# One transformer chain on one core: where the perceptron loop turns, who makes two chunks' low parts, and two small reorderings

## The chip, the core and the metric

One Trainium2 chip, one NeuronCore. The metric is the device time of one execution in microseconds (us). The work of a core is spread over TensorE (PE in the profile; its weight loads are PEld), VectorE (DVE), ScalarE (ACT), GpSimd (POOL) and SyncE (SP, which here only issues DMAs). They run side by side and wait for each other on semaphores.

## The reference

Two blocks of two layers each, 512 latent tokens (and 256 context tokens in the first block), width 1024, all in float32. Cut to what the change touches:

```python
# first block, layer i: attention (neighbourhood, then sliding window), then
h = h + ga1 * (attention(modulate(rms_norm(h, g), sh1, sc1)) @ wo)
h = h + ga2 * (jnp.square(jax.nn.relu(modulate(rms_norm(h, g), sh2, sc2) @ w1)) @ w2)
# second block, layer 0 (even mixer): differential attention y_a and an mLSTM y_b
hm = mlstm_chunkwise(q, k, v, i, f) * jax.nn.sigmoid(o)
y_b = rmsnorm(hm, ml_head_g) * jax.nn.silu(z)
h = h + rmsnorm(concat(y_a, y_b) @ w_out, post_g)
```

## The kernel before

The residual stream stays in SBUF as `m.h`, 8 tiles of 128 features by up to 768 tokens. The program is a row of stages, each a block in which every engine has its own stream of instructions, with a barrier of all engines between two of them: a prologue, neighbourhood attention (`na_stage`), the first perceptron (`mlp_stage`, layer 0, 768 tokens), sliding-window attention (`swa_stage`), the second perceptron (`mlp_stage`, layer 1, 512 tokens), differential attention, `mlstm_stage` and `odd_stage`.

**Precision and chunks.** Each big product is three matmuls (`mm3`, L284 to L286): high part by high part, low by high, high by low. So each weight chunk (128 x 2048) is loaded by SP into one of two slots of `raw`; ScalarE copies it to `wh` (`split_hi`, L238: the high part) and GpSimd subtracts (`low_part`, L245, four pieces of 512 columns: `wl = raw - wh`). TensorE waits for the low part. The last two chunks handled in a stage already belong to the stage that follows: at a stage's end the low part of slot 0 was GpSimd's (`coming.low(pool, 0)`, or `split_lo(pool, m, 0, 0)` in `swa_stage`) and that of slot 1 is VectorE's (`coming.low(dve, 1)`, `split_lo(dve, m, 1, 1)`), in the same four pieces.

**The perceptron.** 16 blocks of 256 hidden features. An "up" projection (letters a, b, c, d, in two tiles t = 0, 1) makes `lin[t] = w1 @ u`; ScalarE makes `relu` from it (L740, step `e_g t`) and its square's high part `hid_hi` (L743), VectorE the square (L835) and its low part (L839, step `lo_g t`). A "down" projection (x, y, v, w, eight tiles n) multiplies by `w2`, and VectorE adds each tile to the residual (L848, step `e_g n`). TensorE needs bank `lin[n % 2]` back from two tiles earlier, so up tile t after a down waits for `e_y6`, `e_y7`. The order is a, then seven rounds of b x c y, then d v w.

**Counting steps.** `Steps` turns a step's name into a semaphore value. In a loop it is `i * len(body) + const`, and for a step of the round before (`back = 1`) one body less. In round 0 "the round before" is not there: the value then is whatever lies one body length under the named step.

```python
up("b", i * 4 + 1, 1, i, lambda t: [(A, f"e_a{t}", ()), (D, f"e_y{6 + t}", (i, 1))])
```

VectorE's body has 24 steps and 4 steps ahead of it (`s_a0, lo_a0, s_a1, lo_a1`). So in round 0 the wait for `e_y6` of the round before is a wait for VectorE's third step, `s_a1`, and that for `e_y7` one for the fourth.

**A stage's end** (`Stats`). After the last down (w) or output projection, each residual tile k is squared by ScalarE as soon as VectorE has added to it (L357; from k = 3 on it waits for GpSimd's sum number k - 2, whose buffer it reuses), GpSimd adds squares 1 to 5 (L364), and TensorE sums the sum and squares 6 and 7 over the features with a matrix of ones (`Stats.sum`, L373). ScalarE then splits the chunk in slot 1 and makes the root (L379, L381). TensorE fills up with matmuls that nobody reads (`keep_busy`, L292). Then comes the barrier, and VectorE starts to scale the next stage's input.

**The start of `swa_stage`.** Small projections share two PSUM banks in turn (`Linear`): entry n of the list `order` needs its bank back from entry n - 2. For the first keys: a sum of squares for the norm (`sums`, L2180, freed by ScalarE's `rstd`, L1900), a product with a swap matrix for the rotation (`swaps`, L2186, freed by VectorE's `rotate`, L2001); for the values three projections (`values`, freed by ScalarE, L1909). The attention scores (`scores`) come after two of the three.

**The end of `mlstm_stage`.** Four heads i. TensorE does each head's gates and state, then the output projection of the head before (`project_out(i - 1)`, 8 tiles, added by VectorE in `add`, L3244), then the sum of squares of head i (`sums`, L3442); ScalarE makes the root (L3046), VectorE scales (`output_norm` L3229, `output_scale` L3234), ScalarE takes the high part (L3055), VectorE the low part (L3239). After the last head, `project_out(3)` has nothing in front of it that could run meanwhile.

Of the kernel before, what the change touches and what calls it, by code (L numbers as in the profile page):

```python
# [7 lines left out]
ALU = mybir.AluOpType  # L8
# [8 lines left out]
LAT = 512  # L17
# [414 lines left out]
class Ahead:  # L432
# [251 lines left out]
def mlp_stage(nc, m, layer, tok, rstd, first, second):  # L684
# [4 lines left out]
    with ExitStack() as ctx:  # L689
# [25 lines left out]
        def down(g, pre=""):  # L715
            return [f"{pre}{g}{n}" for n in range(KT)]
        A.plan(up_act("a"), up_act("b") + up_act("c"), rounds, up_act("d"))
        D.plan(up_dve("a"), up_dve("b") + down("x", "e_") + up_dve("c") + down("y", "e_"),
               rounds, up_dve("d") + down("v", "e_") + down("w", "e_"))
        E.plan(up_pe("a"), up_pe("b") + down("x") + up_pe("c") + down("y"), rounds,  # L720
               up_pe("d") + down("v") + down("w"))
        m.G.plan()

        with nc.Block() as block:
# [8 lines left out]
            def _(act):  # L733
                def up(g, par, i, next_chunk, free=None):
                    if free:
                        act.wait_ge(E.sem, E.at(*free))
                        split_hi(act, m, *next_chunk)
# [9 lines left out]
                up("a", 0, None, None)  # L747
                with act.Fori(0, rounds) as i:
                    up("b", 1, i, (2, 4, i), ("y7", i, 1))
                    act.wait_ge(E.sem, E.at("x0", i))  # L750
                    split_hi(act, m, 3, 4, i)
                    up("c", 0, i, (4, 4, i), ("x7", i))
                    act.wait_ge(E.sem, E.at("y0", i))
                    split_hi(act, m, 5, 4, i)
                up("d", 1, None, (4 * rounds + 2, 4, None), ("y7", rounds - 1))
# [17 lines left out]
            def _(pe):  # L773
# [37 lines left out]
                up_first()  # L811
                with pe.Fori(0, rounds) as i:
                    up("b", i * 4 + 1, 1, i, lambda t: [(A, f"e_a{t}", ()), (D, f"e_y{6 + t}", (i, 1))])
                    down_("x", 0, i * 4 + 2, 0, [("lo_a1", ()), ("lo_c1", (i, 1))],
                          lambda n: [(A, f"e_b{n}", (i,))] if n < 2 else [(D, f"e_x{n - 2}", (i,))])
                    up("c", i * 4 + 3, 1, i, lambda t: [(D, f"e_x{6 + t}", (i,))])
                    down_("y", 1, i * 4 + 4, 0, [("lo_b1", (i,))],
                          lambda n: [(A, f"e_c{n}", (i,))] if n < 2 else [(D, f"e_y{n - 2}", (i,))])
                z = rounds - 1
                up("d", 4 * rounds + 1, 1, None, lambda t: [(D, f"e_y{6 + t}", (z,))])  # L820
                down_("v", 0, 4 * rounds + 2, 0, [("lo_c1", (z,))],
                      lambda n: [(A, f"e_d{n}", ())] if n < 2 else [(D, f"e_v{n - 2}", ())])
                down_("w", 1, 4 * rounds + 3, 1, [("lo_d1", ())],
# [6 lines left out]
            def _(dve):  # L830
# [12 lines left out]
                def down_(g, i):  # L843
                    for n in range(KT):
# [6 lines left out]
                        ins.then_inc(*D.mark(f"e_{g}{n}"))  # L851

                norm.dve(dve)
                up("a", 0, None)
                with dve.Fori(0, rounds) as i:
                    up("b", 1, i)
                    down_("x", i)
                    up("c", 0, i)
                    down_("y", i)
                up("d", 1, None)  # L860
# [837 lines left out]
def swa_stage(nc, m, rstd_u):  # L1698
# [3 lines left out]
    with ExitStack() as ctx:  # L1702
# [57 lines left out]
        order += [("q", 0, 4), ("q", 0, 5)] + [("kk", 0, x) for x in range(3, 8)] + [("vv", 0, x) for x in range(3)]  # L1760
# [58 lines left out]
        with nc.Block() as block:  # L1819
# [51 lines left out]
            def _(pool):  # L1871
# [4 lines left out]
                split_lo(pool, m, 0, 0)  # L1876
# [3 lines left out]
            def _(act):  # L1880
# [115 lines left out]
            def _(dve):  # L1996
# [112 lines left out]
                for k in range(KT):  # L2109
                    gated(3, k)  # L2110
                split_lo(dve, m, 1, 1)

            @block.tensor
            def _(pe):
# [740 lines left out]
def mlstm_stage(nc, m, loaded):  # L2855
# [3 lines left out]
    with ExitStack() as ctx:  # L2859
# [60 lines left out]
        for i in range(H):  # L2920
# [3 lines left out]
            order += [("wo", i - 1, n) for n in range(KT)] if i else []  # L2924
            order += [("ss", i)] if i else []
            order += [("q", i + 1), ("k", i + 1)] if i + 1 < H else []
# [16 lines left out]
        with nc.Block() as block:  # L2943
# [179 lines left out]
            def _(dve):  # L3123
# [177 lines left out]
                for i in range(H):  # L3301
# [14 lines left out]
                    if i:  # L3316
                        for k in range(KT):
                            add(i - 1, k)
                    output_norm(i)
# [710 lines left out]
```

## Time and profile before

| | |
|---|---|
| three runs of the kernel | 2924.36, 2929.61, 2930.51 us (median 2929.61) |
| the profiled execution: its own time | 2935.99 us |
| its span, first to last instruction | 2934.1 us |
| mean granted TensorE clock | 0.985 of full |
| busy share of the span | PE 94%, PEld 76%, DVE 45%, ACT 37%, POOL 30% |

The rows of a timeline read: start, duration, engine, line, operation, output and inputs, shape, how many in a row; in brackets how long the engine had stood idle, and whose work ended that. A line is often a helper's: all big matmuls stand on L284 to L286, and the tiles tell what they are (`u_hi` with `w_hi`: an up projection; `hid_hi` with `w_hi`: a down projection).

### The profile page before, as it was taken

The numbers are of one execution on the slowest core, as the hardware profiler recorded it, in microseconds if no ns is written. First come the engines' busy times: TensorE is split into PE (matmuls) and PEld (weight loads), VectorE is DVE, ScalarE is ACT, GpSimd is POOL, SyncE is SP. The second block draws the span as 40 slices with busy tenths as digits, with TensorE's granted clock in tenths as the row PEclk, the third lists the DMA queues.
The fourth block names the chain that finished last, engine by engine and source line by source line (L and its number), as shares of the span: only waits on it lengthen the run. The fifth ranks groups of instructions, "written<-read, shape, count | busy, mean of one in ns | idle before, by whom it ended". The sixth has DMA issues, their size and how long they took to land. (4 is left out here: it accounts for less than half of the span.)

```text
span 2934.1 us, 40211 instructions
## 1 busy us (share of the span) xinstructions
PE 2761.7 (94%) x16006; PEld 2238.1 (76%) x16006; DVE 1332.7 (45%) x2485; ACT 1088.1 (37%) x1838; POOL 869.4 (30%) x668
## 2 busy tenths in 40 slices
PE   5989999889999999899989999999989999899997
PEld 3777778678888888666657878777767888698886
DVE  4334343453333334545654444455554344605554
ACT  3444445442112212455543232344443333443222
POOL 1201111022323324111114444423333243245443
PEclk9999999999999999999999999999999999999999
DMA  5222332211111111222212222221222121122221
GB/s 219 76 104 104 111 116 111 88 44 58 57 71 57 62 67 37 75 87 87 87 44 86 88 98 88 95 64 58 72 72 68 70 72 72 64 97 86 93 94 58
DMA packets 54278, 238.91 MB, mean 81 GB/s; under 512 B 4212, under 2 KB 22132, under 8 KB 29944
## 3 DMA queue, kind: packets, MB, share of 16 engines
q1 hardware_dynamic: 54136, 236.94, 22.6%
q8 instruction: 99, 1.62, 0.2%
q14 instruction: 43, 0.35, 0.0%
HBM read 234.83 MB, written 2.10 MB: 81 GB/s over the span
## 5 line engine op out<-in xcount | busy, mean ns | idle before, releaser
L245 POOL TENSOR_TENSOR w_lo<-w_raw,w_hi 128x512 fp32r<-128x512 f32 x634 | 825.1, 1333 | 2030.2 <-ACT w_hi L238 685.2
L284 PE MATMUL bank<-u_hi,w_hi 128*128 128x512 f32 (+1 forms) x1984 | 746.9, 376 | 30.2 <-POOL w_lo L245 10.6
L285 PE MATMUL bank<-u_lo,w_hi 128*128 128x512 f32 (+1 forms) x1984 | 734.6, 370 | 0.0
L286 PE MATMUL bank<-u_hi,w_lo 128*128 128x512 f32 (+1 forms) x1984 | 733.9, 370 | 0.0
L284 PEld LDWEIGHTS bank<-u_hi,w_hi 128*128 128x128 f32 x1984 | 377.8, 190 | 110.6 <-issue 25.6
L286 PEld LDWEIGHTS bank<-u_hi,w_lo 128*128 128x128 f32 x1984 | 377.5, 190 | 63.8
L285 PEld LDWEIGHTS bank<-u_lo,w_hi 128*128 128x128 f32 x1984 | 378.1, 191 | 62.7 <-issue 1.9
L848 DVE SCALAR_TENSOR_TENSOR resid<-bank,mod,resid 128x512 f32<-128x512 f32 (+1 forms) x384 | 242.4, 659 | 171.4 <-PE bank L286 169.5
L284 PE MATMUL bank<-hid_hi,w_hi 128*128 128x512 f32 (+1 forms) x768 | 276.7, 360 | 3.7 <-DVE resid L848 3.7
L286 PE MATMUL bank<-hid_hi,w_lo 128*128 128x512 f32 (+1 forms) x768 | 273.9, 357 | 0.0
L285 PE MATMUL bank<-hid_lo,w_hi 128*128 128x512 f32 (+1 forms) x768 | 273.2, 356 | 0.0
L238 ACT ACTIVATE w_hi<-w_raw 128x2048 fp32r<-128x2048 f32 x64 | 122.7, 1917 | 308.9 <-PE bank L286 307.0
L835 DVE TENSOR_TENSOR square<-relu 128x768 f32<-128x768 f32 (+1 forms) x64 | 63.6, 994 | 353.6 <-ACT relu L740 353.4
L284 PE MATMUL bank<-w_hi,u_hi 128*128 128x256 f32 x752 | 215.8, 287 | 5.5 <-DVE k_rotated L2001 3.1
L286 PE MATMUL bank<-w_hi,u_lo 128*128 128x256 f32 x752 | 213.4, 284 | 0.0
L285 PE MATMUL bank<-w_lo,u_hi 128*128 128x256 f32 x752 | 213.4, 284 | 0.0
L284 PEld LDWEIGHTS bank<-hid_hi,w_hi 128*128 128x128 f32 x768 | 144.1, 188 | 33.6 <-DVE resid L848 10.4
L740 ACT ACTIVATE relu<-bank 128x768 f32<-128x768 f32 (+1 forms) x64 | 45.2, 706 | 318.3 <-PE bank L286 318.3
L286 PEld LDWEIGHTS bank<-hid_hi,w_lo 128*128 128x128 f32 x768 | 144.8, 189 | 22.1
L285 PEld LDWEIGHTS bank<-hid_lo,w_hi 128*128 128x128 f32 x768 | 144.3, 188 | 22.3
L284 PEld LDWEIGHTS bank<-w_hi,u_hi 128*128 128x128 f32 x752 | 144.9, 193 | 11.5 <-issue 9.0
L285 PEld LDWEIGHTS bank<-w_lo,u_hi 128*128 128x128 f32 x752 | 145.0, 193 | 0.4 <-issue 0.2
(378 smaller groups left out, 3981.1 us busy)
## 6 DMA issues: line engine op xcount, KB each, us to landing
w_raw<-stream SPq DMA_DIRECT2D x184, 1024.0 KB, 4.8
w_raw<-stream SPq DMA_DIRECT2D x44, 512.0 KB, 4.4
bias<-bias SPq DMA_DIRECT2D x8, 896.0 KB, 6.7
ada_more<-stream SPq DMA_DIRECT2D x4, 1024.0 KB, 11.6
resid<-h SPq DMA_DIRECT2D x1, 3072.0 KB, 10.1
out<-resid SPq DMA_DIRECT2D x8, 256.0 KB, 2.0
w_raw<-stream SPq DMA_DIRECT2D x4, 256.0 KB, 4.4
cos_sin<-cst SPq DMA_DIRECT2D x1, 512.0 KB, 5.8
```

Of the source, the lines that this page charges most:

```text
L238: act.activation(m.wh[:, s, 0:width], m.raw[:, s, 0:width], ACT.Copy).then_inc(m.hi_split, 1)
L245: ins = eng.tensor_tensor(m.wl[:, s, w], m.raw[:, s, w], m.wh[:, s, w].bitcast(F32), ALU.subtract)
L284: pe.matmul(out, lh, rh, start=start, stop=False)
L285: pe.matmul(out, lh, rl, start=False, stop=False)
L286: return pe.matmul(out, ll, rh, start=False, stop=stop)
L740: act.activation(relu[:, par, t, :], m.lin[t][:, 0:tok], ACT.Relu).then_inc(*A.mark(f"e_{g}{t}"))
L835: dve.tensor_tensor(square[:, t, :], relu[:, par, t, :], relu[:, par, t, :], ALU.mult).then_inc(*D.mark(f"s_{g}{t}"))
L848: ins = dve.scalar_tensor_tensor(out=m.h[:, n, a:b], in0=m.lin[n % 2][:, a:b], scalar=m.mod[:, layer, 5, n, w:w + 1], in1=m.h[:, n, a:b], ...
```

## The change

- **Perceptron.** The rounds are turned by one projection: a and b ahead of the loop, seven rounds of x c y d, then v and w. The order of the projections is the same. What is written differently is the waits: b, now outside, waits for `e_a` alone; x waits for `e_b` and for `e_d` of the round before; y for `lo_b1` and for `lo_d1` of the round before. In round 0 these last values are those of `e_b0`, `e_b1` and `lo_b1`, which x and y wait for anyway.
- **Low parts.** In both perceptrons and in `swa_stage` the four pieces of the low part of slot 0 move from GpSimd to VectorE, one piece after each of four residual tiles: after tiles 2 to 5 of w, and after tiles 1 to 4 of the last output projection of `swa_stage`. GpSimd then only has the five additions of squares. (`mlstm_stage` keeps its low part on GpSimd.)
- **`swa_stage`, start.** `values(0)` comes before the second key's sum and swap, on TensorE, on ScalarE and in the list of banks.
- **`mlstm_stage`, last head only.** The sum of squares comes after six tiles of the output projection of head 2 instead of after all eight; VectorE does four of its additions before `output_norm`, two after, and two after the low part.

```diff
@@ class Ahead
+    def low_quarter(self, eng, s, x):
+        m, n = self.m, self.width(s) // 4
+        w = slice(x * n, x * n + n)
+        if x == 0:
+            eng.wait_ge(*self.hi.at(s + 1))
+        ins = eng.tensor_tensor(m.wl[:, s, w], m.raw[:, s, w], m.wh[:, s, w].bitcast(F32), ALU.subtract)
+        if x == 3:
+            ins.then_inc(self.lo.sem)
@@ mlp_stage
-        E.plan(up_pe("a"), up_pe("b") + down("x") + up_pe("c") + down("y"), rounds,
-               up_pe("d") + down("v") + down("w"))
+        E.plan(up_pe("a") + up_pe("b"), down("x") + up_pe("c") + down("y") + up_pe("d"), rounds,
+               down("v") + down("w"))
...
                 split_lo_loop(pool, m, 8, [CHUNK] * 4, last=True)
-                coming.low(pool, 0)
                 after.add(pool)
...
                 up_first()
+                up("b", 1, 1, None, lambda t: [(A, f"e_a{t}", ())])
                 with pe.Fori(0, rounds) as i:
-                    up("b", i * 4 + 1, 1, i, lambda t: [(A, f"e_a{t}", ()), (D, f"e_y{6 + t}", (i, 1))])
                     down_("x", 0, i * 4 + 2, 0, [("lo_a1", ()), ("lo_c1", (i, 1))],
-                          lambda n: [(A, f"e_b{n}", (i,))] if n < 2 else [(D, f"e_x{n - 2}", (i,))])
+                          lambda n: [(A, f"e_b{n}", ()), (A, f"e_d{n}", (i, 1))] if n < 2 else [(D, f"e_x{n - 2}", (i,))])
...
                         ins.then_inc(*D.mark(f"e_{g}{n}"))
+                        if g == "w" and 2 <= n < 6:
+                            coming.low_quarter(dve, 0, n - 2)
@@ swa_stage
-                split_lo(pool, m, 0, 0)
                 after.add(pool)
...
-                for p in range(3):
-                    rstd(("kk", 0), p)
+                rstd(("kk", 0), 0)
                 values(0)
+                rstd(("kk", 0), 1)
+                rstd(("kk", 0), 2)
...
                 swaps(("kk", 0), 0)
+                values(0)
                 sums(("kk", 0), 1)
                 swaps(("kk", 0), 1)
                 sums(("kk", 0), 2)
-                values(0)
                 values(1)
@@ mlstm_stage
-                    if i:
+                    if i and i + 1 < H:
                         project_out(i - 1)
-                    if i:
                         sums(i)
+                    if i + 1 == H:
+                        project_out(i - 1, range(6))
+                        sums(i)
+                        project_out(i - 1, range(6, KT))
```

How the instructions stand now, at the three places that matter most. TensorE at the first up projection b of the first perceptron; the names in brackets are the semaphores waited for. Before:

```order
L286 MATMUL bank<-u_hi,w_lo 128x256
L812 UNCONDITIONAL_BRANCH
L812 ISA
L791 ISA [waits scalar_steps,lo_split]
L284 MATMUL bank<-u_hi,w_hi 128x512 [waits vector_steps]
L285 MATMUL bank<-u_lo,w_hi 128x512
```

and now:

```order
L285 MATMUL bank<-u_lo,w_hi 128x256
L286 MATMUL bank<-u_hi,w_lo 128x256
L284 MATMUL bank<-u_hi,w_hi 128x512 [waits scalar_steps,lo_split]
L285 MATMUL bank<-u_lo,w_hi 128x512
L286 MATMUL bank<-u_hi,w_lo 128x512
```

The entry of the loop and the wait on VectorE's steps are gone from this place; the loop's entry now stands before x.

TensorE at the start of `swa_stage`. Before:

```order
L2180 MATMUL bank<-s,cst_sb 128x512 [waits swa_squared,swa_lin_free1]
L2186 MATMUL bank<-v,cst_sb 128x512 [waits swa_lin_free1,swa_lin_free0]
L2180 MATMUL bank<-sq,cst_sb 128x512 [waits swa_squared,swa_lin_free1]
L2186 MATMUL bank<-x,cst_sb 128x512 [waits swa_lin_free0]
L2180 MATMUL bank<-sq,cst_sb 128x512 [waits swa_squared,swa_lin_free1]
L2186 MATMUL bank<-x,cst_sb 128x512 [waits swa_lin_free0]
L2180 MATMUL bank<-sq,cst_sb 128x512 [waits swa_squared,swa_lin_free1]
L284 MATMUL bank<-w_hi,u_hi 128x256 [waits swa_lin_free0,swa_chunk_lo]
```

and now (L2201 and L2207 are the lines of `sums` and `swaps`; between the two parts stand the 48 matmuls of `values(0)`):

```order
L2201 MATMUL bank<-sq,cst_sb 128x512 [waits swa_squared,swa_lin_free1]
L2207 MATMUL bank<-x,cst_sb 128x512 [waits swa_lin_free0]
L284 MATMUL bank<-w_hi,u_hi 128x256 [waits swa_lin_free1,swa_chunk_lo]
...
L2201 MATMUL bank<-sq,cst_sb 128x512 [waits swa_squared,swa_lin_free0]
L2207 MATMUL bank<-x,cst_sb 128x512 [waits swa_lin_free0,swa_lin_free1]
L2201 MATMUL bank<-sq,cst_sb 128x512 [waits swa_squared,swa_lin_free0]
L284 MATMUL bank<-w_hi,u_hi 128x256 [waits swa_lin_free1]
```

The first value projection now stands between the first key's swap and the second key's sum.

VectorE in the last down projection of the second perceptron, now (L859 is the addition to the residual, L848 before; L469 is the subtraction of `low_quarter`):

```order
L859 SCALAR_TENSOR_TENSOR resid<-bank,mod,resid 128x512 [waits vector_steps,tensor_steps] x11
L469 TENSOR_TENSOR w_lo<-w_raw,w_hi 128x512 [waits late_ahead_hi]
L859 SCALAR_TENSOR_TENSOR resid<-bank,mod,resid 128x512 [waits vector_steps,tensor_steps]
L469 TENSOR_TENSOR w_lo<-w_raw,w_hi 128x512
L859 SCALAR_TENSOR_TENSOR resid<-bank,mod,resid 128x512 [waits vector_steps,tensor_steps]
L469 TENSOR_TENSOR w_lo<-w_raw,w_hi 128x512
L859 SCALAR_TENSOR_TENSOR resid<-bank,mod,resid 128x512 [waits vector_steps,tensor_steps]
L469 TENSOR_TENSOR w_lo<-w_raw,w_hi 128x512
L859 SCALAR_TENSOR_TENSOR resid<-bank,mod,resid 128x512 [waits vector_steps,tensor_steps] x2
```

Before, the 16 additions of v and w stood in one unbroken row; now four subtractions stand among the last six.

## Rows read from the trace of the kernel before

**Rows 1.** Who waited for whom on PE: total us, times, longest

```profile
PE bank L373 <- POOL resid L364: 6.2, 4, 3.1
PE bank L284 <- DVE square L835: 6.0, 2, 3.7
...
PE bank L292 <- PEq L2943: 2.7, 1, 2.7
```

**Rows 2.** Timeline, first perceptron: first relu on ACT, start of b on PE

```profile
639.18 0.81 ACT L740 ACTIVATE relu<-bank 128x768 f32<-128x768 f32 x1 [2.02 <-PE bank L286]
...
643.16 0.50 PE L284 MATMUL bank<-u_hi,w_hi 128*128 128x512 f32 x1 [3.66 <-DVE square L835]
```

**Rows 3.** Timeline, second perceptron: the same two

```profile
1540.03 0.60 ACT L740 ACTIVATE relu<-bank 128x512 f32<-128x512 f32 x1 [2.62 <-PE bank L286]
...
1543.00 0.50 PE L284 MATMUL bank<-u_hi,w_hi 128*128 128x512 f32 x1 [2.33 <-DVE square L835]
```

**Rows 4.** Sums by window: busy us (count) per engine, then PEclk, DMA

```profile
1224.80:1228.20 3.40, 3.40 (x18) 3.40 (x17) 1.21 (x3) 0.00 (x0) 0.00 (x0) 0.50 0.37 154
1228.20:1231.60 3.40, 3.40 (x31) 3.40 (x30) 0.00 (x0) 0.60 (x1) 0.00 (x0) 1.00 0.02 5
...
1893.00:1899.00 6.00, 5.05 (x8) 2.28 (x9) 2.50 (x4) 3.22 (x4) 0.90 (x1) 0.72 0.00 0
2508.00:2516.00 8.00, 5.01 (x14) 4.01 (x15) 2.57 (x4) 3.48 (x3) 4.49 (x4) 0.57 0.00 0
643.20:649.00 5.80, 5.80 (x19) 4.60 (x20) 0.96 (x1) 1.05 (x1) 4.68 (x4) 0.71 0.01 3
```

**Rows 5.** Timeline, start of `swa_stage`, PE, ACT and DVE

```profile
1216.20 1.12 PE L2180 MATMUL bank<-sq,cst_sb 128*128 128x512 f32 x2 [0.58 <-ACT sq L1900]
1218.16 1.13 PE L2186 MATMUL bank<-x,cst_sb 128*128 128x512 f32 x2 [0.84 <-DVE k_rotated L2001]
...
1223.28 0.36 PE L284 MATMUL bank<-w_hi,u_hi 128*128 128x256 f32 x1 [3.14 <-DVE k_rotated L2001]
...
1215.48 0.67 ACT L1900 ACTIVATE sq<-bank,misc 128x512 f32<-128x512 f32 x1
...
1222.46 0.68 DVE L2001 TENSOR_TENSOR k_rotated<-bank,cos_sin 128x512 f32<-128x512 f32 x1
```

**Rows 6.** Timeline, same place: one DVE form with and without POOL beside it

```profile
1215.65 6.33 POOL L245 TENSOR_TENSOR w_lo<-w_raw,w_hi 128x512 fp32r<-128x512 f32 x4 [1.72 <-ACT w_hi L1885]
...
1220.96 1.57 DVE L2009 TENSOR_TENSOR k_rotated<-k_rotated,sq 128x512 f32<-128x512 f32 x1
...
1224.64 0.69 DVE L2009 TENSOR_TENSOR k_rotated<-k_rotated,sq 128x512 f32<-128x512 f32 x1
```

**Rows 7.** Timeline, end of the second perceptron

```profile
1881.88 5.06 POOL L245 TENSOR_TENSOR w_lo<-w_raw,w_hi 128x512 fp32r<-128x512 f32 x4 [5.12 <-ACT w_hi L461]
1886.91 6.99 POOL L364 TENSOR_TENSOR resid<-resid 128x512 f32<-128x512 f32 x5
...
1893.95 4.43 PE L373 MATMUL bank<-resid,cst_sb 128*128 128x512 f32 x6 [3.11 <-POOL resid L364]
...
1896.45 2.50 DVE L245 TENSOR_TENSOR w_lo<-w_raw,w_hi 128x512 fp32r<-128x512 f32 x4 [4.82 <-ACT w_hi L461]
1900.40 1.41 DVE L508 SCALAR_TENSOR_TENSOR z<-resid,vec_sb 128x512 f32<-128x512 f32 x2 [1.44 <-PEq L724]
```

**Rows 8.** Timeline, ends of `swa_stage` and of the first perceptron, PE's sums

```profile
1520.52 4.33 PE L373 MATMUL bank<-resid,cst_sb 128*128 128x512 f32 x6 [2.07 <-POOL resid L364]
...
1169.52 4.14 PE L373 MATMUL bank<-relu,cst_sb 128*128 128x512 f32 x12
```

**Rows 9.** Timeline, end of `mlstm_stage`: root, scaling, last output projection

```profile
2505.93 0.69 ACT L3046 ACTIVATE rstd<-bank,misc 128x512 f32<-128x512 f32 x1 [3.96 <-PE bank L3442]
...
2510.99 0.77 PE L284 MATMUL bank<-u_hi,w_hi 128*128 128x512 f32 x1 [5.09 <-issue]
```

**Rows 10.** Instructions of line 855, VectorE's loop in the perceptrons: ns min/median/max

```profile
L855 DVEq COMPARE_BRANCH  x14: 50/56/68, 712.9 to 1857.6; - x14
```

More of the change, by code:

```diff
@@ L733, in _, with up @@
             def _(act):
[L734 to L737, printed above, removed]
+                def up(g, par, i):
                     for t in range(2):
@@ L859, in _ @@
                     down_("y", i)
-                up("d", 1, None)
+                    up("d", 1, i)
                 down_("v", None)
@@ L1759, in swa_stage @@
         order = [("q", 0, 0), ("q", 0, 1), ("kk", 0, 0), ("q", 0, 2), ("q", 0, 3), ("kk", 0, 2), ("kk", 0, 1)]
-        order += [("q", 0, 4), ("q", 0, 5)] + [("kk", 0, x) for x in range(3, 8)] + [("vv", 0, x) for x in range(3)]
+        order += [("q", 0, 4), ("q", 0, 5), ("kk", 0, 3), ("kk", 0, 4), ("vv", 0, 0)]
+        order += [("kk", 0, x) for x in range(5, 8)] + [("vv", 0, 1), ("vv", 0, 2)]
         for u in range(PAIRS * TILES):
@@ L2110, in _ @@
                     gated(3, k)
+                    if k == 1:
+                        dve.wait_ge(m.hi_split, m.s0 + 1)
+                    if 1 <= k < 5:
+                        w = slice((k - 1) * LAT, k * LAT)
+                        ins = dve.tensor_tensor(m.wl[:, 0, w], m.raw[:, 0, w], m.wh[:, 0, w].bitcast(F32), ALU.subtract)
+                    if k == 4:
+                        ins.then_inc(m.lo_split, 1)
                 split_lo(dve, m, 1, 1)
@@ L2923, in mlstm_stage @@
             order += [("den", i), ("num", i, 0), ("num", i, 1)]
-            order += [("wo", i - 1, n) for n in range(KT)] if i else []
+            sum_at = 6 if i + 1 == H else KT
+            order += [("wo", i - 1, n) for n in range(sum_at)] if i else []
             order += [("ss", i)] if i else []
+            order += [("wo", i - 1, n) for n in range(sum_at, KT)] if i else []
             order += [("q", i + 1), ("k", i + 1)] if i + 1 < H else []
@@ L3316, in _ @@
                     if i:
-                        for k in range(KT):
+                        for k in range(KT if i + 1 < H else 4):
                             add(i - 1, k)
                     output_norm(i)
+                    if i + 1 == H:
+                        add(i - 1, 4)
+                        add(i - 1, 5)
                     if i == 0:
@@ L3326, in _ @@
                     low_y(i)
+                    if i + 1 == H:
+                        add(i - 1, 6)
+                        add(i - 1, 7)
                     if i and i + 1 < H:
@@ L3443, in sums, with project_out @@
                     ins.then_inc(lin_done.sem)
-                def project_out(i):
+                def project_out(i, tiles=range(KT)):
                     pe.wait_ge(*lower(fill["wo", i]))
@@ L3448, in project_out @@
                     wh, wl = columns(m.wh, "wo", i), columns(m.wl, "wo", i)
-                    for k in range(KT):
+                    for k in tiles:
                         n, c = use["wo", i, k], slice(k * P, k * P + P)
```

30 lines of the change are left out of this document (18 added, 12 removed).

## The prediction

> **What bounds the kernel.** I read the page first (PE is busy for 94% of the span, no other engine for half), so time is won only where TensorE stands still or runs slowly. Then the list of what PE waited for [rows 1]: two waits for VectorE's square at L835, 6.0 us together, and four for GpSimd's additions at L364, 6.2 us. Then the timeline around each gap at the places of the diff. What to see there:
>
> The first projection b of each perceptron starts late. Its bank is free when ScalarE's relu ends, at 639.18 + 0.81 = 639.99 and at 1540.03 + 0.60 = 1540.63, yet PE starts at 643.16 and 1543.00, released by the square [rows 2, 3]. That is the wait for a "round before" that isn't there.
>
> A gap costs twice when the clock falls behind it. A stretch at granted clock c loses (1 - c) of its length: 5.8 us at 0.71 after the first gap are 1.7 us; 3.4 us at 0.50 at the start of the sliding window are 1.7 by this rule, and 13 matmuls of 0.12 = 1.5 by the count (18 done, where the next 3.4 us hold 31) [rows 4]. These are the levels 1.2 and 2.4 GHz.
>
> At the start of the sliding window PE stands for 0.58, 0.84 and 3.14 us behind the key rotation, while the value projections, which need none of it, are queued behind [rows 5].
>
> At the ends of the second perceptron and of the sliding-window stage PE waits 3.11 and 2.07 us for GpSimd, which began its five additions only after its own low part [rows 7, 8]. At the end of the first perceptron it doesn't wait [rows 8].
>
> At the end of the mLSTM stage PE stands for 5.09 us behind root, scaling and high and low part of the last head [rows 9].
>
> **Part by part**, against the profiled execution (2935.99 us; the median of the three runs is 2929.61, 6.4 lower; I subtract the same sum from it).
>
> *1. First b, first perceptron.* New start: 639.99 + 0.06 for the semaphore = 640.05 instead of 643.16, so 3.1 us. The gap left, about 0.6 us, is like the 0.58 and 0.84 in [rows 5], behind which the clock stayed whole, so the 1.7 us of [rows 4] go as well: **4.8**. Behind it nothing is late: chunk 2 has its low part ready 7 us before x needs it.
>
> *2. First b, second perceptron.* 1540.69 instead of 1543.00: **2.3**. There was no slow clock behind this one.
>
> *3. The loop's new turn.* A turn is a branch of 0.056 us and some register work [rows 10], about 0.45 us together. On VectorE it now stands between the low part of d and the first addition of x, and in the second perceptron that chain does hold PE up at x2 already. But the sequencer does it while the subtraction runs (0.69 us). Taken at 0; bounds 0 and, fully exposed, 12 turns of 0.45 = 5.4 lost.
>
> *4. Start of the sliding window.* `values(0)` can begin when ScalarE has freed its bank, 1215.48 + 0.67 = 1216.15 [rows 5], so the 0.58 stay. It fills 48 x 0.12 = 5.8 us, to 1222.0. By then the bank of the first swap is long free: the second key's sum follows at once, its swap behind it (ScalarE has copied the values by then), the last sum at 1223.9, `values(1)` at about 1224.8, when VectorE, free from 1222.5, has read the swap. It ends at 1230.6, where before it ended at 1236.4. In terms: 0.84 and 3.14 of idle and 1.5 of slow clock are gone, 0.1 lost on handovers: **5.4**. VectorE still has to finish the second key (about 3.5 us from 1224.1); scores come at 1230.6, so 2.9 us are left over.
>
> *5. The low parts on VectorE.* First what the trace shows of the two engines side by side: the same operation with two SBUF inputs took 0.69 us alone and 1.57 with GpSimd busy, and GpSimd's four pieces took 6.33 instead of 5.06 [rows 6, 7]. A piece of `low_quarter` has two SBUF inputs as well. The additions to the residual, with one input in PSUM, take 0.75 in either case. VectorE lost 0.88, less than one piece of GpSimd (5.06 / 4 = 1.27), and three of GpSimd's pieces lost 0.42 each (6.33 - 5.06 over three). So I take an alternation: each quarter waits for the addition that GpSimd has begun, and GpSimd's next one for the quarter. Of the 0.42 the handover between two additions hides a part: (6.99 - 1.27) / 4 = 1.43 from one to the next, 0.15 of it idle; 0.28 are left. The Trainium skill ("SBUF — State Buffer", section "SBUF: two separate sides") states that this pair of ports is an exclusive lock held for a whole instruction and that the later one blocks fully. By that rule no operation is slowed once it has begun, and the trace agrees with it, since the 1.57 is the 0.69 with a wait in front.
>
> Second perceptron: the first addition can start when square 1 is there, at 1884.1 (the addition to tile 1 at 1882.64, 0.75, and the square, 0.63); five end 4 x 1.43 + 1.3 later, at 1891.1, and four delays of 0.28 make 1892.3; VectorE, with 0.66 + 0.6 per tile of 1.37, is late by half a us at the end. PE's sums begin 1.6 us earlier, and at full clock (1.7 in [rows 4]) the root comes 3.2 earlier. But the stage can't end before VectorE's low part of slot 1: last square 1893.1, high part 1.9, low part 2.5, barrier 0.3 = 1897.8 instead of 1900.40 [rows 7]: **2.6**. Sliding window, where the first quarter still finds GpSimd idle: the same steps give 1525.0 instead of 1527.1: **2.1**. First perceptron: GpSimd's additions there end at 1169.5, just when PE is done, so an earlier start buys nothing, and the lock moves them by 0.2: **-0.2**.
>
> Bounds of the three tails: with no lock at all 3.4, 2.5 and 0. With every quarter at 1.57 in VectorE's queue a tile takes 0.66 + 1.57 = 2.23 instead of 1.37, four of them are 3.4 us late, and the tails give about 0, -0.9 and -2.0. I stay near the upper end, since only the wait for GpSimd's rest is added, not a whole piece each time.
>
> *6. mLSTM end.* The sum of squares starts when ScalarE's square is done, 2502.0 instead of 2504.01; root at 2503.97 instead of 2505.93. VectorE is then the later one: four additions, `output_norm`, two additions to 2505.5, against 2507.3 before; scale 1.2, high part 1.1, low part 1.2 as before. The last output projection starts at 2509.2 instead of 2510.99: 1.8. The two tiles moved behind the sum cut PE's gap to 2.6 us, and gaps of 2.3 to 2.6 left the clock up elsewhere, while 3.1 and more brought it down. Then 8 us at 0.57 [rows 4] lose their part with PE at work, 2.0. GpSimd's low part and five additions end at 2521.8 at the earliest, VectorE's low part after them at 2526.9, with barrier 2527.2 instead of 2530.1: **2.9**; if the clock falls as before, 1.7.
>
> Sum: 4.8 + 2.3 + 0 + 5.4 + 2.6 + 2.1 - 0.2 + 2.9 = **19.9 us**. 2935.99 - 19.9 = 2916.1 for a profiled execution, **2909.7** against the median. PE is the bound after each place, so I let nothing of it be given back.
>
> **The rivals.**
>
> *A. The lock at its full price.* The tails give -2.9 instead of 4.5, the sum is 12.5: 2917.1. For it: 1.57 is the common value in [rows 6], and in the tails GpSimd is never idle. Against it: VectorE has 0.1 to 0.4 us per tile to spare, and PE only needs a bank two tiles later.
>
> *B. The clock falls all the same*, at the first b (1.7), at the sliding window (1.5) and in the mLSTM (1.2): 4.4 less, 2914.1. For it: the 2.07 us gap in [rows 8] was followed by a slow stretch too. Against it: the gaps left at the first two places are under 0.8 us.
>
> *C. It is given back, or a wait stays.* If the head start of the sliding window were lost in its 32 units, for instance at a chunk whose load is not moved: 5.4 less, 2915.1. Or the first b keeps some other wait. For it: PE already waits 1.3 us for a load in that stage. Against it: the loads hang on low parts, which move along.
>
> *D. The turn costs, and the kernel is slower.* The loop now turns where the next instruction needs the last one's result soon. The price, if a turn empties a queue, is bounded by PE's longest wait for its own sequencer, 2.7 us at a stage's start [rows 1]. 12 turns at 2.7 are 32.4, less 19.9 is 12.5 slower: 2942.1. It decides from 1.7 us per turn on (19.9 / 12), and passes 0.2% at 2.2. Against it: the loop turned before as well, 14 branches of 0.05 us with the next register work 0.15 us later, and PE showed no step at its turn. The Trainium skill ("Runtime: NRT & Kernel Launch", section "Instruction fetch mechanics") states that a taken branch to code that isn't in the fetched pages stalls for a DMA. By that rule the turn would cost in its new place as soon as the work queued ahead of it is short; no row here shows such a stall.
>
> **How the numbers follow.** Main case 0.62, A 0.12, B 0.15, C 0.08, D 0.03. About 0.2% (5.9 us) is what a measurement of this kernel can tell from no change. The main case, A, B and C all lie over it, 12.5 us or more; I leave 0.03 for a mixture that doesn't. Faster 0.93, same 0.03, slower 0.04 (D and the unforeseen). The range: upwards A with the spread of the runs (3 us), 2920; downwards the main case without lock (1.1), and the spread, with some slow stretches fewer: 2903.
>
> **What would show it right or wrong.** In the new profile PE should start b about 0.6 us after a in the first perceptron and 0.2 in the second, with no wait named L835's successor; the clock should be whole after it. In `swa_stage` the first value projection should begin 0.6 to 0.7 us after the first key's swap and scores about 5.5 us sooner after the stage's start. The quarters in the tails should take 1.0 to 1.4 us, not 0.69; PE's wait for GpSimd should be under 1 us, and the stage should end on VectorE's low part. The last output projection of the mLSTM should wait 2.4 to 2.7 us. Wrong it is if a PE gap appears at each turn, if tiles of w come more than 1 us late, or if a later stage waits longer for loads.

## The result and the profile after

| | before | after |
|---|---|---|
| median of the runs | 2929.13 us (4 runs) | 2909.57 us (2907.39 to 2912.56, 4 runs) |
| ratio, with its 95% interval | | 0.9933 (0.9921 to 0.9945) |
| profiled execution, its own time | 2935.99 us | 2909.22 us |
| its span | 2934.1 us | 2907.5 us |
| mean granted clock | 0.985 | 0.984 |

The medians differ by 19.6 us; 19.9 were forecast. A second set of six runs, beside eleven of the kernel before, gave 0.9943 (0.993 to 0.9956), with medians 16.8 us apart.

The two profiled executions differ by more, 26.8 us, so the traces must be read with care: some of that isn't the change's. First the waits of PE, in the list that answers to [rows 1] (engine, line and what it waited for: us in total, times, longest). Line numbers moved: L859 was L848, L846 was L835, L2966 was L2943.

```profile
PE bank L284 <- issue: 8.9, 5, 2.5
...
PE bank L284 <- DVE resid L859: 4.1, 15, 0.6
...
PE bank L373 <- POOL resid L364: 2.9, 4, 1.6
```

The wait for the square, 6.0 us in two, is gone from the list, and the wait for GpSimd's additions is 2.9 us instead of 6.2. Then the places of the change, in the timeline (start, duration, engine, line, operation; in brackets the idle time before and who ended it). The first projection b in the two perceptrons, which answers to [rows 2, 3]:

```profile
634.07 0.81 ACT L747 ACTIVATE relu<-bank 128x768 f32<-128x768 f32 x1 [2.02 <-PE bank L286]
...
635.03 0.47 PE L284 MATMUL bank<-u_hi,w_hi 128*128 128x512 f32 x1 [0.64 <-ACT relu L747]
...
1525.79 0.47 PE L284 MATMUL bank<-u_hi,w_hi 128*128 128x512 f32 x1
```

0.64 us instead of 3.66, and 0.1 (the row shows no idle time) instead of 2.33. Start of `swa_stage`, which answers to [rows 5]: the sum, the swap, and the value projection right behind it.

```profile
1204.18 1.02 PE L2201 MATMUL bank<-sq,cst_sb 128*128 128x512 f32 x2
1205.13 1.12 PE L2207 MATMUL bank<-x,cst_sb 128*128 128x512 f32 x2
1206.93 0.36 PE L284 MATMUL bank<-w_hi,u_hi 128*128 128x256 f32 x1 [0.68 <-ACT sq L1913]
```

Ends of the stages, which answer to [rows 7 to 9]: PE's sum in the first perceptron, in the sliding window, where the next two rows are VectorE's low part of slot 1 and the first work behind the barrier, and in the mLSTM stage, after the last output projection.

```profile
1160.13 1.12 PE L373 MATMUL bank<-relu,cst_sb 128*128 128x512 f32 x2 [0.37 <-POOL relu L364]
...
1506.36 2.84 PE L373 MATMUL bank<-resid,cst_sb 128*128 128x512 f32 x6 [0.36 <-POOL resid L364]
...
1509.29 2.50 DVE L245 TENSOR_TENSOR w_lo<-w_raw,w_hi 128x512 fp32r<-128x512 f32 x4 [2.50 <-ACT w_hi L238]
1512.10 1.41 DVE L518 SCALAR_TENSOR_TENSOR relu<-resid,gsc 128x512 f32<-128x512 f32 x2 [0.32 <-PEq L1833]
...
2483.95 0.47 PE L284 MATMUL bank<-u_hi,w_hi 128*128 128x512 f32 x1 [2.51 <-issue]
...
2496.65 2.81 PE L373 MATMUL bank<-resid,cst_sb 128*128 128x512 f32 x6 [1.56 <-POOL resid L364]
```

The clock is whole where it had fallen (rows of windows: PE busy with its count, granted clock, DMA): behind the first b and at the start of the sliding window, which answers to [rows 4].

```profile
635.60:641.40 5.80, 5.80 (x30) 1.00 0.01 3
1207.00:1213.00 6.00, 6.00 (x49) 1.00 0.37 124
```

To see where the 26.8 us come from, I laid PE's instructions of the two traces side by side, one by one, and followed by how much the same instruction starts earlier. The lead grows where time is won:

| stretch | lead at its end | won here | forecast |
|---|---|---|---|
| prologue and neighbourhood attention (not changed) | 5.1 | 5.1 | 0 |
| first b, first perceptron | 9.8 | 4.65 | 4.8 |
| its tail | 9.4 | -0.4 | -0.2 |
| start of the sliding window | 15.0 | 5.6 | 5.4 |
| its 32 units (not changed) | 13.2 | -1.8 | 0 |
| its tail, to the barrier | 15.0 | 1.8 | 2.1 |
| first b, second perceptron | 17.2 | 2.3 | 2.3 |
| its seven rounds | 16.9 | -0.35 | 0 |
| its tail | 19.4 | 2.5 | 2.6 |
| differential attention and mLSTM up to its last head (not changed) | 25.4 | 6.0 | 0 |
| end of the mLSTM | 28.2 | 2.85 | 2.9 |
| last stage (not changed) | 26.7 | -1.5 | 0 |

The changed stretches hold 19.0 us against 19.9; the other four hold 7.8 us, and they are the reason why two single executions differ by more than the medians. The lead of the changed stretches isn't free of such accidents either: the experiments below show where. Two examples from the unchanged ones. In the prologue the same sixteen matmuls take 1.93 us in the trace before and 1.07 in the trace after:

```profile
33.77 1.93 PE L534 MATMUL bank<-w_raw,silu_c 128*32 128x256 f32 x16
```

```profile
32.81 1.07 PE L544 MATMUL bank<-w_raw,silu_c 128*32 128x256 f32 x16
```

And in the differential attention and the mLSTM the granted clock fell to 0.50 for other lengths in the same work. Windows of before, then of the same work after:

```profile
1958.60:1968.80 10.20, 9.30 (x23) 0.50 0.39 104
2470.60:2477.40 6.80, 6.80 (x15) 0.50 0.22 67
```

```profile
1939.20:1949.40 10.20, 9.26 (x34) 0.83 0.39 104
2447.50:2454.30 6.80, 6.80 (x27) 1.00 0.10 22
```

### The profile page after: what moved, and what is told of

The parts are those of the page before. It is cut to its first block and busy times, and to the rows that moved or that the text cites. A ratio compares the mean times of both kernels' runs of the same rounds, so it can differ in the third digit from the quotient of the medians.

```text
span 2907.5 us, 40224 instructions
## 1 busy us (share of the span) xinstructions
PE 2746.8 (94%) x16006; PEld 2229.7 (77%) x16006; DVE 1345.3 (46%) x2497; ACT 1087.8 (37%) x1838; POOL 857.3 (29%) x656
## 5 line engine op out<-in xcount | busy, mean ns | idle before, releaser
L245 POOL TENSOR_TENSOR w_lo<-w_raw,w_hi 128x512 fp32r<-128x512 f32 x622 | 811.1, 1337 | 1948.5 <-ACT w_hi L238 638.1
L859 DVE SCALAR_TENSOR_TENSOR resid<-bank,mod,resid 128x512 f32<-128x512 f32 (+1 forms) x384 | 242.2, 659 | 163.9 <-PE bank L286 161.9
L846 DVE TENSOR_TENSOR square<-relu 128x768 f32<-128x768 f32 (+1 forms) x64 | 64.5, 1007 | 344.9 <-ACT relu L747 344.7
```

Of the source, the lines that this page charges most:

```text
L245: ins = eng.tensor_tensor(m.wl[:, s, w], m.raw[:, s, w], m.wh[:, s, w].bitcast(F32), ALU.subtract)
L846: dve.tensor_tensor(square[:, t, :], relu[:, par, t, :], relu[:, par, t, :], ALU.mult).then_inc(*D.mark(f"s_{g}{t}"))
L859: ins = dve.scalar_tensor_tensor(out=m.h[:, n, a:b], in0=m.lin[n % 2][:, a:b], scalar=m.mod[:, layer, 5, n, w:w + 1], in1=m.h[:, n, a:b], ...
```

## The experiments

### Each part alone

The first four kernels are the kernel before with one part of the change each; the edits are the diff's hunks of that part.

**The turned loops** (the hunks of `mlp_stage` but for the quarters).

> The kernel before with the turned perceptron loops alone. The prediction's terms 1 to 3 say 4.8 + 2.3 + 0 = 7.1 us faster: ratio 0.9976. In the trace, PE's first projection b starts 0.6 us after a in the first perceptron and with no gap over 0.5 us in the second, with no stretch at the low clock behind it, and no PE gap at the loop's turn. If the clock falls all the same, 5.4 us faster. Rival (the turn costs): each of the 14 turns shows a PE gap that the kernel before does not have, and the gain is under 7.1 by the sum of them; at 0.45 us each for 12 turns the gain is 1.7 us, at 2.7 us each the kernel is 25 us slower.

Measured: 0.9964 (0.9952 to 0.9977), 2920.48 us beside 2929.51. The spread of the kernel before was 2920.36 to 2933.48 there, so the lead in the traces says more: 4.6 us at the first b, 2.3 at the second, and 0.4 lost over the seven rounds of the second perceptron, 6.5 in all. The 0.4 isn't the turn's: against the same trace of before, the third and fourth kernel below, whose loops are not turned, lose 0.4 and 0.35 us over the same rounds, in the same even steps of about 0.03 us. The stretch simply lasts 0.1% longer in some executions.

```profile
636.07 0.47 PE L284 MATMUL bank<-u_hi,w_hi 128*128 128x512 f32 x1 [0.64 <-ACT relu L737]
```

**The low parts** (`low_quarter`, its four calls in `down_("w")`, the four pieces in `swa_stage`, without GpSimd's).

> The kernel before with VectorE's quarters of the low part in the three tails alone. Alternation of the two engines (the prediction): 2.6 + 2.1 - 0.2 = 4.5 us faster, ratio 0.9985; but the trace of the whole change shows tiles of 1.70 us instead of 1.37 and 1.40 while the quarters and GpSimd's additions alternate, which takes about 0.8 us in each short tail, so 3 to 4.5. Rival (full price of the lock, 1.57 us for each quarter in VectorE's queue): 2.9 us slower. Rival (no lock): 5.9 us faster, with quarters of 0.69 us.

Measured: 0.9987 (0.9977 to 0.9997), that is 3.8 us. In the traces: -0.4 in the first perceptron, 1.8 in the sliding window, 2.5 in the second perceptron, 3.9 together. Neither rival: it is the alternation.

A part of the last two numbers is the clock and not the overlap. In the kernel before, PE's waits of 2.07 and 3.11 us for GpSimd are followed by a granted clock of 0.50 for 3.4 us, and the two tails (from one of PE's last output matmuls to VectorE's first work behind the barrier) take 18.35 and 14.30 us. In the trace of the fourth kernel below the same two tails, with the same waits, kept the whole clock and took 17.15 and 13.17. With the quarters they take 16.6 and 11.8, and the clock stayed whole there in all seven traces that have them. So about 1.2 and 1.1 us of the 1.8 and 2.5 are low clock that no longer comes.

**The start of the sliding window** (`values(0)` ahead of the second key).

> The kernel before with the sliding-window stage's first value projection moved alone. The prediction's term 4 says 5.4 us faster, ratio 0.9982: gaps of 0.84 and 3.14 us gone and no low clock behind them. Rival (given back inside the stage's 32 units): the stage's end comes less than 1 us earlier after its start than before, and the time is the same within 1 us. Rival (the clock falls all the same): 3.9 us.

Measured: 0.9967 (0.9954 to 0.998). In the traces 5.6 us at this place. Behind it the lead falls again, by 2.1 us over the stage's units, where the granted clock was 0.50 from 1363.6 to 1367.0 and from 1462.6 to 1466.0 us (in the trace before only once, from 1364.7 to 1368.1). That isn't the head start given back: from 1232 us on, the units last 276.7 us in the trace before, 278.8 here, and 278.2 and 278.5 in the second and fourth kernel, whose start is as before. The ratio says 9.7 us and the medians 7.8, more than the trace has at the place.

**The mLSTM's last head** (the hunks of `mlstm_stage`).

> The kernel before with the split of the last head's output projection alone. The prediction's term 6 says 2.9 us faster, ratio 0.9990, with the clock whole behind a gap of 2.4 to 2.7 us; 1.7 us if the clock falls behind it as before. Rival (VectorE's four additions ahead of the scaling eat the gain): the last output projection starts less than 0.5 us earlier after the stage's last unit, and the time is the same within 1 us.

Measured: 0.9993 (0.9984 to 1.0002), 2.1 us, which alone couldn't be told from nothing. In the traces 2.8 us, with the gap of 2.51 ahead of the last output projection and the clock whole behind it. The end of the kernel before was a slow one in its trace, with the clock low for 6.8 us; in three other traces with the old mLSTM end it was low for 3.4 us and the stage's end came 0.45 us sooner. Against those the gain is 2.3 us.

The four leads make 18.8 us, the whole change 19.0 in its trace: the parts don't disturb each other by more than some tenths. (The 0.4 us lost in the rounds of the first kernel and the 0.35 lost in those of the whole change have different places, so that the sums agree this well is partly luck.) The four ratios make about 26 us, which shows how little the median of five to eleven executions says of 3 us here.

### The false wait put back into the turned loop

```diff
-                up("b", 1, 1, None, lambda t: [(A, f"e_a{t}", ())])
+                up("b", 1, 1, None, lambda t: [(A, f"e_a{t}", ()), (D, ("s_a1", "lo_a1")[t], ())])
```

> The turned loops of the first experiment, but the first projection b, now outside the loop, waits as before for VectorE's square and low part of a1. If only the false wait cost and the turn is free (the prediction), PE's gap ahead of b is back at 3.66 us in the first perceptron and 2.33 in the second with the low clock behind the first, both perceptrons last as long as in the kernel before, and nothing else moves. Rival (part of the 4.8 and 2.3 us came from the loop's new turn, or the turn costs and hides a part of the gain): the perceptrons' loops are longer or shorter than before by more than 0.3 us.

Measured: one run, 2925.26 us, beside one of the kernel before of 2924.19. The gaps are back:

```profile
638.63 0.47 PE L284 MATMUL bank<-u_hi,w_hi 128*128 128x512 f32 x1 [3.75 <-DVE square L837]
```

```profile
1538.53 0.47 PE L284 MATMUL bank<-u_hi,w_hi 128*128 128x512 f32 x1 [2.42 <-DVE square L837]
```

The low clock behind the first is back too (0.50 from 640.0 to 643.4 us). So the wait was the whole of terms 1 and 2. The low clock follows the first b in all five traces that have the wait and in none of the seven that don't. The first perceptron runs as long as before to 0.1 us, the second loses 0.5 us against it over its seven rounds, in even steps. Kernels whose loops are not turned lose 0.35 to 0.4 us in those rounds too, and the whole change loses nothing in them behind the first x, so no price of the turn can be read from it.

### GpSimd's additions cut to one column

```diff
+    few = False
+
+    def some(self, t):
+        return t[:, 0, 0:1] if self.few else t
...
-            pool.tensor_tensor(self.acc, self.acc, self.sq[k % 2], ALU.add).then_inc(self.m.st_added.sem)
+            pool.tensor_tensor(self.some(self.acc), self.some(self.acc), self.some(self.sq[k % 2]), ALU.add).then_inc(self.m.st_added.sem)
@@ swa_stage
         after = late_stats(m)
+        after.few = True
```

> The changed kernel with GpSimd's five additions of squares at the end of the sliding-window stage cut to one column each, so that VectorE's four quarters there meet almost no work of GpSimd (the sums of squares of that stage are left out, and the later layers compute with other numbers). If the quarters are long only because GpSimd holds the port, all four take 0.68 to 0.70 us instead of 0.68, 1.27, 1.12 and 1.11, and the output tiles follow each other at 1.40 us instead of 1.70; PE's sum starts 1.0 us earlier or more. Rival (something else slows VectorE there, the PSUM reads or ScalarE's squares): quarters stay over 1.0 us and the tiles at 1.70.

Measured: one run. This kernel leaves out most of a sum of squares, and so computes other numbers; only the rows at this place are compared.

The end of the sliding-window stage on VectorE, in the changed kernel (additions to the residual L2077, quarters L2129):

```profile
1497.54 0.68 DVE L2129 TENSOR_TENSOR w_lo<-w_raw,w_hi 128x512 fp32r<-128x512 f32 x1
1498.27 0.75 DVE L2077 SCALAR_TENSOR_TENSOR resid<-bank,mod,resid 128x512 f32<-128x512 f32 x1
1498.94 1.27 DVE L2129 TENSOR_TENSOR w_lo<-w_raw,w_hi 128x512 fp32r<-128x512 f32 x1
1500.13 0.74 DVE L2077 SCALAR_TENSOR_TENSOR resid<-bank,mod,resid 128x512 f32<-128x512 f32 x1
1500.79 1.12 DVE L2129 TENSOR_TENSOR w_lo<-w_raw,w_hi 128x512 fp32r<-128x512 f32 x1
1501.84 0.74 DVE L2077 SCALAR_TENSOR_TENSOR resid<-bank,mod,resid 128x512 f32<-128x512 f32 x1
1502.50 1.11 DVE L2129 TENSOR_TENSOR w_lo<-w_raw,w_hi 128x512 fp32r<-128x512 f32 x1
```

and on GpSimd at the same time:

```profile
1498.36 3.00 POOL L364 TENSOR_TENSOR resid<-resid 128x512 f32<-128x512 f32 x2 [43.46 <-ACT resid L357]
1501.61 1.45 POOL L364 TENSOR_TENSOR resid<-resid 128x512 f32<-128x512 f32 x1 [0.25 <-ACT resid L357]
```

With one column per addition (L2083 and L2135 are the same two lines):

```profile
1503.48 0.75 DVE L2083 SCALAR_TENSOR_TENSOR resid<-bank,mod,resid 128x512 f32<-128x512 f32 x1
1504.15 0.68 DVE L2135 TENSOR_TENSOR w_lo<-w_raw,w_hi 128x512 fp32r<-128x512 f32 x1
1504.88 0.75 DVE L2083 SCALAR_TENSOR_TENSOR resid<-bank,mod,resid 128x512 f32<-128x512 f32 x1
1505.55 0.68 DVE L2135 TENSOR_TENSOR w_lo<-w_raw,w_hi 128x512 fp32r<-128x512 f32 x1
```

GpSimd's additions are 0.19 us long there instead of 1.28 to 1.56. All quarters are 0.68, the tiles follow at 1.40 us instead of 1.71 (1500.13 to 1501.84), and from the sum of the stage before to this one it is 344.9 us instead of 346.2: 1.3 us. So the long quarters, and the slower tiles, come from GpSimd's additions and not from the PSUM reads or from ScalarE's squares, which are still there. The rows above show the two engines taking turns. GpSimd's second addition ends at 1501.36, and the quarter that began meanwhile ends 0.55 us later, at 1501.91; the next addition began meanwhile and ends 1.15 us after that, at 1503.06. Each is its own duration (0.68 and 1.30) behind the other's end, less 0.13 to 0.15. With the rule of the Trainium skill ("SBUF — State Buffer", section "SBUF: two separate sides"), a lock held for a whole instruction, these rows agree but for these 0.15 us.

### Quarters earlier, halves for the high part, both

The last four kernels ran together on one chip, with the changed kernel as it is among them.

> The changed kernel once more, beside the next three on one chip. The clock falls at other places from run to run in the prologue, in the differential attention and in the mLSTM stage, so its time against the kernel before should again be 17 to 22 us less, 0.9933 within 0.001, and the profile should show the same gains at the places of the change (4.6, 5.6, 1.8, 1.9, 2.5 and 2.9 us) whatever the rest does.

Measured: 2911.62 us, 0.9943 (0.993 to 0.9956), and the stage lengths of its trace equal those of the first one within 0.1 us but for the prologue and the part from the differential attention to the end of the mLSTM, as expected.

```diff
-                        if g == "w" and 2 <= n < 6:
-                            coming.low_quarter(dve, 0, n - 2)
+                        if g == "w" and n < 4:
+                            coming.low_quarter(dve, 0, n)
@@ mlstm_stage
-                coming.low(pool, 0)
                 post.add(pool)
...
                 for k in range(KT):
                     add(H - 1, k)
+                    if k < 4:
+                        coming.low_quarter(dve, 0, k)
```

(and in `swa_stage` after tiles 0 to 3 instead of 1 to 4).

> The changed kernel with VectorE's quarters two tiles earlier in the perceptrons and one tile earlier in the sliding-window stage, so that one or two of them run before GpSimd's first addition, and with the mLSTM stage's low part of slot 0 as four quarters on VectorE too. The alternation of the two engines costs about 0.4, 0.8 and 0.7 us in the three tails; half of it should go (0.9 us together), and in the mLSTM stage GpSimd starts its additions 1.1 us earlier, so PE's wait of 1.56 us falls to about 0.4: 2 us faster than the changed kernel. Rival (the quarter delays the addition to the residual and the square behind it, so that what the additions gain the tiles lose): within 0.5 us of it.

Measured: 2909.65 us, 0.9934 (0.9922 to 0.9947): 2.0 us under the changed kernel beside it, which the overlapping intervals can't tell from nothing. In the traces 0.3 to 0.4 us at each of the first three tails and 0.5 in the mLSTM, 1.5 together where 2 were expected. Two quarters of the second perceptron now come ahead of GpSimd:

```profile
1870.51 0.68 DVE L469 TENSOR_TENSOR w_lo<-w_raw,w_hi 128x512 fp32r<-128x512 f32 x1
...
1871.88 0.68 DVE L469 TENSOR_TENSOR w_lo<-w_raw,w_hi 128x512 fp32r<-128x512 f32 x1
...
1873.26 1.30 DVE L469 TENSOR_TENSOR w_lo<-w_raw,w_hi 128x512 fp32r<-128x512 f32 x1
...
1875.14 1.11 DVE L469 TENSOR_TENSOR w_lo<-w_raw,w_hi 128x512 fp32r<-128x512 f32 x1
```

The three tails gave what was expected (half of the cost of the alternation), the mLSTM didn't: PE still waits 1.07 us for the additions there, not 0.4.

```diff
@@ class Ahead, high and low of slot 1 where it has 2048 columns; the same in swa_stage
-        act.activation(self.m.wh[:, s, w], self.m.raw[:, s, w], ACT.Copy).then_inc(self.hi.sem)
+        for x in range(parts):
+            n = self.width(s) // parts
+            w = slice(x * n, x * n + n)
+            act.activation(self.m.wh[:, s, w], self.m.raw[:, s, w], ACT.Copy).then_inc(self.hi.sem)
```

> The changed kernel with ScalarE's high part of the chunk in slot 1 in two halves at the ends of the sliding-window, second perceptron and mLSTM stages, VectorE's low part of the first half beside the second. If those stages end on VectorE's low part, as the profile of the changed kernel reads, each ends 0.7 to 0.9 us earlier, 2.5 us together; then the root (which is done 0.7 to 1.2 us before the low part now) sets the end. Rival (the root waits behind ScalarE's longer high part and is late itself): no gain.

Measured: 2906.82 us, 0.9928 (0.9913 to 0.9942), 4.8 us under the changed kernel beside it. The traces show about half of that: the sliding window's end wins 0.85 us, the second perceptron's 0.8, the mLSTM's 0.75, so 2.4 where 2.5 were expected. VectorE starts its low part in the middle of ScalarE's high part (second perceptron; ACT, then DVE):

```profile
1875.04 1.99 ACT L465 ACTIVATE w_hi<-w_raw 128x1024 fp32r<-128x1024 f32 x2
```

```profile
1876.11 2.50 DVE L483 TENSOR_TENSOR w_lo<-w_raw,w_hi 128x512 fp32r<-128x512 f32 x4 [1.64 <-ACT w_hi L465]
```

So these stages did end on VectorE's low part, as the prediction said.

> The two variants before this together: 4.5 us faster than the changed kernel, 24 us faster than the kernel before, ratio to it 0.992. If the earlier sum moves the root forward, the halves are worth their full 2.5 us here even if less alone.

Measured: 2907.35 us, 0.9926 (0.9914 to 0.9938). It is 4.3 us under the changed kernel beside it, and the best ratio of all, though it can't be told from the halves alone by these runs. Its trace has the gains of both at the first three tails: 0.4, 1.15 and 1.2 us. At the mLSTM's end the granted clock fell to 0.50 right behind the last gap (2486.8 to 2490.2 us), and what both win there is hidden by it: the stage ends 0.1 us later than in the first trace of the changed kernel, and 0.8 sooner than in the second, where the clock fell at the same place.

## Why the prediction was right

The time, 2909.57 us against 2909.7, fits better than the parts deserve: the second set of runs has its medians 16.8 us apart and not 19.6, so agreement to 0.1 us is luck. What isn't luck is that the parts fit, each at its own place.

*Terms 1 and 2* are right in size and cause: 4.65 and 2.3 us against 4.8 and 2.3. The wait put back brings them back.

*Term 3* was taken at 0, and the turns cost nothing that the traces can show: behind the first x, the second perceptron's rounds last as long as before within 0.1 us in five of the six traces of kernels with the whole change, and within 0.25 in the sixth; the first perceptron's within 0.1 in all. What is lost is 0.35 us at the first x alone, where VectorE starts the low part of b1 0.46 us after its square instead of 0.10. It is in every kernel with the whole change and in neither kernel with only the loops turned; what it is stays open.

```profile
1538.75 0.69 DVE L850 TENSOR_TENSOR hid_lo<-square,hid_hi 128x512 fp32r<-128x512 f32 x1 [0.46 <-DVE square L846]
```

*Term 4*: 5.6 against 5.4, with the low clock at the stage's start in all five traces of the old order and in none of the seven of the new. The term's own steps put the end of `values(1)` at 1230.6 instead of 1236.4, which is 5.8 us and not 5.4; the measured value lies between the two workings.

*Term 5* has the right mechanism and nearly the right sizes: 2.5, 1.8 and -0.4 us against 2.6, 2.1 and -0.2. (Its bound without a lock is 3.4 + 2.5 + 0 = 5.9, which is 1.4 us over the 4.5 of the main case; the range was worked out with 1.1.) The quarters took 1.11 to 1.32 us where GpSimd was at work, inside the 1.0 to 1.4 that were named. But the working has VectorE "late by half a us at the end" in one place only; in truth it holds up PE's tiles in all three tails (1.70 us instead of 1.37 in the second perceptron and 1.40 in the sliding window, 2.26 instead of 2.12 in the first), because 0.66 + 1.04 us of work don't fit beside such a tile.

*Term 6*: 2.85 against 2.9 (2.3 against the three other traces of the old end), with 2.51 us ahead of the last projection where 2.4 to 2.7 were named. One reason given for it was wrong: "gaps of 2.3 to 2.6 left the clock up elsewhere, while 3.1 and more brought it down". In the second trace of the same kernel the clock fell 1.5 us behind that very gap:

```profile
2482.90:2486.30 3.40, 3.40 (x10) 0.50 0.00 0
```

while in the first it was whole there:

```profile
2485.50:2488.90 3.40, 3.40 (x17) 1.00 0.00 0
```

So whether the forecast was right on that point depends on the execution that one looks at, and that the clock held in the first is luck; the difference is about 1 us.

*The rivals.* A (full price) is out: 3.9 us won by that part alone. B did not happen at the first b nor behind the gap of 0.68 us at the start of the sliding window in any trace with the change; in the mLSTM it happened in three of seven. (A low stretch some 20 us ahead of that start stands in four of the twelve traces, two with the old order and two with the new; it costs 1.5 us.) C is out: the units of the sliding window last as long in kernels whose start wasn't changed (276.6 to 278.5 us) as in those where it was (276.9 to 278.9), and the differences lie where the clock fell. D is out: even the 0.5 us of the kernel with the false wait put back would be 0.5 / 7 = 0.07 us for a turn, where 1.7 was needed, and it isn't the turn's.

*The six us* between the profiled execution of before and its median were treated as an offset to carry along. That was safe here: the leads put 7.8 us of the difference between the two profiled executions into stages that the change doesn't touch.

## What to carry to other kernels

A wait for "the round before" in a counted loop must be read for round 0: what it names there may be a step that is just about to happen, and taking it out cost nothing here. Where VectorE and GpSimd both work on operands in SBUF, sort their operations in time rather than by load: a quarter took 0.68 us ahead of GpSimd's first addition and 1.1 to 1.3 beside them. And when an execution's clock can wander by several us, compare the same instruction's start in both traces, not the medians of parts: the leads of the four parts added up to 18.8 of 19.0 us, their ratios to 26. One trace of before isn't enough for tenths of a microsecond, though: what looked like a price of the turned loop, 0.4 us, stood in the traces of kernels that turn nothing.

## What the runs showed of the hardware

- The low clock comes in other stretches in each execution of the same program. From the sum at the end of the second perceptron to that at the end of the mLSTM it took 621.2 and 618.8 us in the two traces of the changed kernel and 630.6 in that of the kernel before, of which the change accounts for some 3. What decides it stays open, but the twelve traces can be counted. Behind these gaps of PE the granted clock fell to 0.50:

| PE's gap and its place | traces with a low clock behind it |
|---|---|
| 0.64, first b; 0.68, start of the sliding window (after) | 0 of 7; 0 of 7 |
| 2.1, end of the sliding window (before) | 4 of 5 |
| 2.33 to 2.42, first b, second perceptron (before) | 1 of 5 |
| 2.51, last output projection (after) | 3 of 7 |
| 3.1, end of the second perceptron (before) | 4 of 5 |
| 3.14, start of the sliding window (before) | 5 of 5 |
| 3.66 to 3.75, first b, first perceptron (before) | 5 of 5 |
| 5.09, last output projection (before) | 5 of 5 |

- In the prologue of before, PE's matmuls took 1.93 us instead of 1.07 per sixteen while the granted clock of that stretch reads 1.00. In the kernel with the low parts alone the same sixteen took 1.93 us too, and there the clock reads 0.50 (before, then that kernel):

```profile
32.50:41.50 9.00, 9.00 (x66) 1.00 0.33 119
```

```profile
22.50:56.50 34.00, 24.50 (x141) 0.50 0.62 225
```

  The trace of before holds no record of the clock until 57.4 us, so its 1.00 is no reading at all, and durations have to be read beside the clock.
- VectorE and GpSimd slow each other at a place nobody moved: since b starts earlier in the second perceptron, its square and low part fall onto GpSimd's low part of the next chunk, and take 1.50 and 1.59 us instead of 0.69, while GpSimd's four pieces take 5.48 instead of 5.06. PE doesn't wait for them there.

```profile
1532.16 1.50 DVE L846 TENSOR_TENSOR square<-relu 128x512 f32<-128x512 f32 x1 [3.41 <-ACT relu L747]
1533.77 1.59 DVE L850 TENSOR_TENSOR hid_lo<-square,hid_hi 128x512 fp32r<-128x512 f32 x1
...
1529.34 5.48 POOL L245 TENSOR_TENSOR w_lo<-w_raw,w_hi 128x512 fp32r<-128x512 f32 x4 [23.03 <-ACT w_hi L238]
```
